# Token gather and scatter of a mixture-of-experts step: one-hot picks in f32 replaced by rounded high and low parts

## The chip, the cores and the metric

The kernel runs on one core of a Trainium2 chip. The metric is the device time of one execution in microseconds (us). Before the change, three runs gave 1468.37 us as the median, from 1468.09 to 1469.5.

## What is computed

One inference step of a two-layer decoder for two request groups that share weights: a prompt of 256 tokens and eight single sample tokens, so 264 tokens in all (T = 264), with 1024 features each. Layer 0 is a gated MLP with a causal mixing over chunks, layer 1 a differential attention; behind each stands a mixture of 16 experts, of which a token uses two. Every part ends in a residual and a layer norm. The part that matters here, cut from the reference:

```
h = x * (1 + sc2) + sh2                                   # modulation from a conditioning vector
scores = softmax(h @ router_w);  sel = scores + router_bias
# the group of 4 experts whose two best sel sum highest; in it the two best experts
gate = the two scores, divided by their sum, at their experts; 0 elsewhere     # (264, 16)
a = silu(h @ w_gate[e]) * (h @ w_up[e]) * gate[:, e]      # for every expert e, width 512
f = sum over e of a @ w_down[e]
x = layer_norm(alpha * x + (1 + g2) * f)
```

All inputs and outputs are float32.

## The kernel before

Activations stand with features on the partitions: a tensor such as `hT` is 128 x 8 x 264, eight blocks of 128 features. TensorE (PE) makes products into PSUM, ACT copies them out, VectorE (DVE) does the elementwise work, SyncE (SP) issues the weight loads, GpSimd (POOL) little. Each engine has its own program, written out by hand in its order; counters on semaphores order the engines among themselves. No planner takes part.

**Rounded products.** TensorE's f32 matmul has two matmul rows in the trace; a matmul of two rounded operands (the type fp32r) has one. Wherever weights are multiplied, the kernel splits both operands into a rounded high part, which ACT makes by a copy into a rounded tile, and a rounded low part, which DVE makes as the difference, and adds three products: high x high, high x low, low x high. The gather and the scatter of the experts don't do so: they are f32.

**Stages of one expert layer** (`moe`, in each engine's program). The modulation writes `hT`. TensorE makes the router's logits (L563), transposes them, computes the tile of one later modulation vector (`ada_tile`, L490), and turns `hT` into token rows by transposes (`turned`, L402), six groups of up to four blocks, which ACT copies to `tokA`. Meanwhile DVE selects the experts. From the selection TensorE counts the tokens of each expert by small matmuls (`small`, L425), and so each token gets two slots among 2 x 264 = 528: the slots are sorted by expert. `ada_turn` (L425 too) puts the columns of a finished modulation vector on the partitions; ahead of the gather two such turns run in each layer, and in layer 0 a tile `ada_tile(1, 0, 2)` between them.

DVE makes the one-hot table `pick` (L1689 and L1693): for token t and slot s it is 1 where s is one of t's slots. The *gather* (L599 to L603) multiplies token rows by `pick` in 16 groups, two halves of the slots times eight feature blocks; a group is three f32 matmuls over 128, 128 and 8 tokens, with 264 columns. Its result `xg` holds the features of every slot in expert order, with padding behind.

The experts run in a loop, two to a turn (L659 to L664), each over 128 slots from its first one on. For an expert `part` makes the gate and up products (L620, rounded, in four quarters), DVE and ACT the gated activation, TensorE turns it (L422), and `down` (L639, f32) the down projection of the expert before; ACT copies the result to `yg`, feature blocks by slots. `yg` lies in the buffer `reg2`, which POOL clears at the start of the layer (L1100 to L1103). The weights stream through a ring of six slots of 2 MB (`wring`), which SP loads in one fixed order, each as soon as the slot's last reader is done.

If an expert had more than 128 tokens, all engines would run a further loop (`more_pe` L687, its counterparts on ACT, DVE and SP); every engine reads a flag to a register and branches (on TensorE L691 and L692, on DVE L1604). With the inputs here the body is skipped.

*The tail of the layer.* Behind the last down projection stand, in this order: the wait for ACT, the flag and branch, the transposes of each token's two slot numbers and two gates (`sg`, L422), four spreads of those rows over all partitions (L425) that DVE copies to `sgB`, ten `turned` groups that turn `yg` into slot rows (L402), which ACT copies to `yr`, in layer 0 the tile `ada_tile(1, 1, 0)`, and the *scatter* (L682 to L684): eight groups of five f32 matmuls, over four times 128 and once 16 slots, slot rows times the table `put`. DVE builds `put` in fifteen operations (L1764 to L1771): per block of 128 slots, the gate where the slot is the token's first, plus the gate where it is the second.

```
put[:, k, :] = (sgB[:, 0, :] == mine) * sgB[:, 2, :]
rs[:]        = (sgB[:, 1, :] == mine) * sgB[:, 3, :]
put[:, k, :] = put[:, k, :] + rs[:]
```

Then come in layer 0 one modulation turn and one tile, the residual (DVE scales `xT` first, L1491), and the norm: a sum over features by matmuls (L457), centring (L1510), squares by ACT and their sum, scaling. In layer 0 a turn and a tile lie between the two sums, and DVE does two weight splits of the next projection (`tile_split`, L1477, 2048 elements each) between centring and scaling. That projection, `kv` in layer 0, is L391 with three rounded products per block.

Helpers that these steps share: `group` (L381) opens one of the PSUM banks `pj` and runs a list of matmuls, `evac` on ACT (L1129) copies a bank out, `low` and `high` split expert weights (L1702 on DVE, L1233 on ACT), L1738 multiplies the two halves of an expert's activation.

## Time and profile before

| | |
|---|---|
| runs, median (lowest to highest) | 1468.37 us (1468.09 to 1469.5) |
| the profiled execution, its own time | 1468.32 us |
| its span, from first to last instruction | 1466.5 us |
| TensorE busy | 1273.1 us, 87% of the span |
| VectorE busy | 815.9 us, 56% |
| ScalarE busy | 549.8 us, 37% |
| GpSimd busy | 21.2 us, 1% |
| chain that ended last, by engine | PE 74%, DVE 16%, ACT 3%, issue 2%, DMA 2%, SPq 2% |

Shares of busy time are means over stages of different kinds, so the stages have to be read one by one. The chain of waits follows the work back from the last instruction, at each step to what released it; "issue" in it is time in which an engine waited for nothing that the profile shows. PEclk in a stretch is the granted TensorE clock as a share of 2.4 GHz: 1.00 is 2.4 GHz and 0.50 is 1.2 GHz, values between are stretches with both. An engine's name with a q at its end is its sequencer, PEld the weight loads of TensorE.

### The profile page before, as it was taken

What the parts mean: (1) busy time and instruction counts of PE and PEld (TensorE: products, weight loads), DVE (VectorE), ACT (ScalarE), POOL (GpSimd) and SP (SyncE); (2) the same over time, 40 slices, a digit from 0 to 9 for tenths busy, and PEclk for the clock granted to TensorE, in tenths of its full rate; (3) what the DMA queues carried; (4) which work ended last, traced back from release to release, by engine and by line L of the source; (5) the groups of instructions that cost most, each with busy time, mean ns of one, the idle gap of its engine ahead of it and who ended that gap; (6) DMA issues with size and microseconds to landing.
All of it is one profiled execution on the core that took longest, in us unless ns stands there. A gap on an engine that the chain in (4) does not pass through costs nothing.

```text
span 1466.5 us, 19316 instructions
## 1 busy us (share of the span) xinstructions
PE 1273.1 (87%) x7246; PEld 997.5 (68%) x7246; DVE 815.9 (56%) x970; ACT 549.8 (37%) x663; POOL 21.2 (1%) x26
## 2 busy tenths in 40 slices
PE   4797879899999997899877886676998999999985
PEld 1695745788888885599543443264657888888864
DVE  1436472666666632645599989366316666666334
ACT  1333224555555522353322221133125555555321
POOL 2000010000000000000000000001000000000000
PEclk9899979999999998999856556678559999999988
DMA  9939530999999966534469999853009999999200
GB/s 332 387 114 337 177 111 19 347 336 338 340 338 338 339 235 235 180 125 158 179 222 341 353 342 346 301 214 116 1 0 342 336 337 335 334 335 335 108 2 30
DMA packets 143713, 355.40 MB, mean 242 GB/s; under 512 B 4706, under 2 KB 4899, under 8 KB 143652
## 3 DMA queue, kind: packets, MB, share of 16 engines
q1 hardware_dynamic: 142388, 350.98, 67.4%
q0 software_dynamic: 1264, 3.59, 0.8%
q8 instruction: 40, 0.66, 0.2%
q14 instruction: 21, 0.17, 0.0%
HBM read 351.28 MB, written 3.28 MB: 242 GB/s over the span
## 4 chain that ended last, share of the span: by engine, by line
PE 74%; DVE 16%; ACT 3%; issue 2%; DMA 2%; SPq 2%; ACTq 0%; DVEq 0%
PE gu L620 24%; PE pj L391 20%; PE pj L639 16%; DVE reg L1843 3%; PE tb L425 3%; DVE wring L1840 3%; PE gu L457 2%; PE gu L807 2%; PE tb L422 2%; PE gu L809 1%; DMA wring<-in_a_w_in 1%; SPq L912 1%; PE pj L490 1%; DVE yT L1851 1%; PE pj L402 1%
## 5 line engine op out<-in xcount | busy, mean ns | idle before, releaser
L1702 DVE TENSOR_TENSOR wlo<-wring,whi 128x2048 fp32r<-128x2048 f32 x128 | 290.2, 2289 | 103.7 <-ACT whi L1233 103.6
L1233 ACT ACTIVATE whi<-wring 128x2048 fp32r<-128x2048 f32 x128 | 244.7, 1916 | 144.5 <-PE gu L620 144.5
L639 PEld LDWEIGHTS pj<-tokB,wring 128*128 128x128 f32 x2048 | 233.4, 192 | 4.7 <-issue 2.1
L639 PE MATMUL pj<-tokB,wring 128*128 128x128 f32 x2048 | 233.9, 275 | 1.7 <-issue 1.7
L1129 ACT ACTIVATE reg<-pj 128x264 f32<-128x264 f32 (+2 forms) x168 | 83.9, 510 | 365.2 <-PE pj L391 147.6
L620 PE MATMUL gu<-whi,xhi 128*128 128x512 f32 x512 | 207.7, 406 | 12.9 <-DVE xlo L1728 12.9
L620 PE MATMUL gu<-wlo,xhi 128*128 128x512 f32 x512 | 204.6, 400 | 0.0
L620 PE MATMUL gu<-whi,xlo 128*128 128x512 f32 x512 | 204.4, 399 | 0.0
L620 PEld LDWEIGHTS gu<-whi,xhi 128*128 128x128 f32 x512 | 98.2, 192 | 35.7 <-DVE xlo L1728 7.9
L620 PEld LDWEIGHTS gu<-whi,xlo 128*128 128x128 f32 x512 | 98.1, 192 | 23.2
L620 PEld LDWEIGHTS gu<-wlo,xhi 128*128 128x128 f32 x512 | 98.1, 192 | 21.6
L1728 DVE TENSOR_TENSOR xlo<-reg,xhi 128x1024 fp32r<-128x1024 f32 x32 | 39.2, 1226 | 115.0 <-ACT xhi L1237 115.0
L391 PE MATMUL pj<-yT,tok 128*128 128x264 f32 (+1 forms) x192 | 79.4, 559 | 0.6 <-issue 0.6
L391 PE MATMUL pj<-yT_rounded,wlo 128*128 128x264 f32 x256 | 74.6, 291 | 0.0
L1840 DVE TENSOR_TENSOR wring<-wring,yT 128x2048 f32<-128x2048 f32 x32 | 73.2, 2288 | 2.0 <-ACT yT L1129 1.5
L1843 DVE TENSOR_REDUCE reg<-wring 128x32 f32<-128x2048 f32 x32 | 73.2, 2286 | 1.1
L490 PE MATMUL pj<-wring,cT 128*32 128x512 f32 x384 | 55.7, 708 | 18.9 <-DMA wring<-in_ada_w 18.0
L391 PEld LDWEIGHTS pj<-yT,tok 128*128 128x128 f32 (+1 forms) x192 | 42.3, 253 | 36.7 <-issue 32.4
L1738 DVE TENSOR_TENSOR tokB<-tokB,gu 128x512 f32<-128x512 f32 x32 | 22.0, 688 | 60.0 <-PE gu L620 60.0
L797 PE MATMUL pj<-wring,reg 128*32 128x512 f32 x256 | 51.9, 963 | 1.6 <-DVE lamx L1901 1.6
L1477 DVE TENSOR_TENSOR wlo<-wring,half_reg 128x2048 fp32r<-128x2048 f32 x14 | 32.1, 2290 | 37.3 <-ACT half_reg L1158 37.3
L1129 ACT ACTIVATE yT<-pj 128x264 f32<-128x264 f32 (+1 forms) x48 | 21.3, 459 | 81.4 <-PE pj L391 75.6
(295 smaller groups left out, 1732.1 us busy)
## 6 DMA issues: line engine op xcount, KB each, us to landing
wring<-in_moe_w_gate SPq DMA_DIRECT2D x32, 2048.0 KB, 9.4
wring<-in_moe_w_up SPq DMA_DIRECT2D x32, 2048.0 KB, 10.0
wring<-in_moe_w_down SPq DMA_DIRECT2D x32, 2048.0 KB, 9.0
wring<-in_ada_w SPq DMA_DIRECT2D x24, 2048.0 KB, 13.8
wring<-in_cache_k SPq DMA_DIRECT2D x64, 512.0 KB, 5.0
wring<-in_cache_v SPq DMA_DIRECT2D x64, 512.0 KB, 5.0
wring<-in_a_w_in SPq DMA_DIRECT2D x4, 2048.0 KB, 19.9
wring<-in_a_w_out SPq DMA_DIRECT2D x2, 2048.0 KB, 16.4
```

Of the source, the lines that this page charges most:

```text
L391: m = pe.matmul(out, lhsT, rhs, start=(j == 0), stop=(j == len(pairs) - 1))
L425: return lambda dst: pe.matmul(dst, lhsT, rhs, start=start, stop=stop)
L490: m = pe.matmul(bank[32 * j:32 * j + 32, 0:512], cT[:, k, :], w[:, k, :], start=(half == 0), stop=(half == 1))
L620: m = pe.matmul(gu[q // 2][:, :], x[:, c, :], w[:, k, :], start=(c == 0 and n == 0), stop=(c == C - 1 and n == 2))
L639: m = pe.matmul(bank[:, i * P:(i + 1) * P], w[:, k, f * P:(f + 1) * P], aT[:, k, :], start=(k == 0), stop=(k == FB - 1))
L797: m = pe.matmul(pj[2 + n][32 * p:32 * p + 32, :], sW[:, s % 4, 4 * k + p, :], wring[:, slot, p * D + n * 512:p * D + (n + 1) * 512], start ...
L1129: act.activation(dst, bank[0:rows, 0:n] if n < 512 or rows < P else bank[:, :].rearrange("p (f n) -> p f n", n=P), func, scale=scale).then ...
L1233: act.activation(whi[q], quarter(wring, q, s), ACT.Copy).then_inc(hi_ready, 1)
L1702: dve.tensor_tensor(quarter(wlo, q, s), quarter(wring, q, s), whi[q].bitcast(F32), ALU.subtract).then_inc(lo_ready, 1)
L1728: dve.tensor_tensor(xlo, xg[:, :, bass.ds(first, P)], xhi.bitcast(F32), ALU.subtract).then_inc(xe_ready, 1)
L1840: link(dve.tensor_tensor(keys.rearrange("p (g n) -> p g n", g=2), keys.rearrange("p (g n) -> p g n", g=2), qbc[:, s % 2:s % 2 + 1, :].to_b ...
L1843: i = dve.tensor_reduce(sS[:, s, g0:g0 + 2, :].rearrange("p g x -> p (g x)").unsqueeze(2), keys.rearrange("p (x d) -> p x d", d=HD), AX.X, ...
```

## The change

*Gather.* ACT copies each pair of blocks of `hT` to a rounded tile `hhi`, and DVE writes the difference to `hlo`. `turned` still turns `hT` itself, and ACT copies these rows to rounded tiles `gR`; six more `turned` groups turn `hlo`, and ACT copies those to `gl` and `gls`. The table `pickR` is rounded (it holds zeros and ones). A group of the gather now has six matmuls, high and low part of each of the three token blocks, all of rounded operands.

*Slot numbers and gates.* The transposes of `sg` and TensorE's read of the flag move ahead of the experts. Slot number and gate of the first choice are spread after the last expert's gate and up products, ahead of its `down`, those of the second choice behind `down`; then comes TensorE's branch. DVE compares the spread rows straight out of PSUM with each partition's slot number: `putR` becomes a rounded table of zeros and ones, and the gate of each slot is summed to a column `gcol`.

*Scatter.* ACT copies the turned slot rows out of PSUM times `gcol`, to rounded tiles `yrR`; DVE makes the low part from the same bank, bank times gate minus `yrR`. `turned` waits for DVE's low part four groups back. A group of the scatter has ten matmuls of rounded operands. The tile `ada_tile(1, 1, 0)` waits for the seventh low part, the scatter for all ten.

*Beside.* POOL's clear of `reg2` waits for the end of the gather, and ACT waits for it after the first expert. In layer 0 the turns and tiles behind the scatter each move one place later: turn 1 and tile 2 between the sums of the norm, turn 2 and tile 3 behind the norm. Of the two weight splits of the next projection, on ACT the first moves ahead of the scatter's fourth eviction and the second behind the norm; on DVE one stays between centring and scaling and the other moves behind the norm and the split of the projection's input. The multi-pass branch's buffer `piece` moves to `ws2`.

```diff
...
...
-yr = reg1[:, 0:NK * D].rearrange("p (k n) -> p k n", n=D)
-pick = yT[:, :, :].rearrange("p c t -> p (c t)")[:, 0:3 * SLOT_N].rearrange("p (j n) -> p j n", n=SLOT_N)
-put = hT[:, :, :].rearrange("p c t -> p (c t)")[:, 0:NK * T].rearrange("p (k t) -> p k t", t=T)
-piece = hT[:, :, :].rearrange("p c t -> p (c t)")[:, 0:2048].rearrange("p (b k n) -> p b k n", b=2, n=P)
+gR = rounded("tokens_high", "tok4", 0, 3 * D).rearrange("p (j n) -> p j n", n=D)
+gl = rounded("tokens_low", "tokB", 0, 2 * D).rearrange("p (j n) -> p j n", n=D)
+gls = rounded("sample_low", "reg2", 0, D)
+hhi = rounded("mod_high", "reg2", 0, C * T).rearrange("p (c t) -> p c t", t=T)
+hlo = sqT
+pickR = rounded("pick_rounded", "yT", 0, 3 * SLOT_N).rearrange("p (j n) -> p j n", n=SLOT_N)
+putR = rounded("put_rounded", "hT", 0, NK * T).rearrange("p (k t) -> p k t", t=T)
+yrR = rounded("rows_high", "reg1", 0, NK * D).rearrange("p (k n) -> p k n", n=D)
+lowA = rounded("rows_low_a", "tok4", 0, 3 * D).rearrange("p (k n) -> p k n", n=D)
+lowB = rounded("rows_low_b", "tokB", 0, 2 * D).rearrange("p (k n) -> p k n", n=D)
+piece = ws2[:, :, :].rearrange("p c t -> p (c t)").rearrange("p (b k n) -> p b k n", b=2, n=P)
 flatB = tokB[:, :, :].rearrange("p b n -> p (b n)")
 aT = flatB[:, 0:512].rearrange("p (f n) -> p f n", n=P)
 atok = flatB[:, 512:1024]
 upT = flatB[:, 1024:1536].rearrange("p (f n) -> p f n", n=P)
-sgB = flatB[:, 0:4 * T].rearrange("p (i t) -> p i t", t=T)
...
+def slots_of(k):
+    return P if k < NK - 1 else LAST
+def row_low(k):
+    return lowA[:, k, :] if k < 3 else lowB[:, k - 3, :]
...
+        at[f"modulated{l}"] = op.n
...
+        operand()
+        for n, j in ((NB, 2), (P, 0), (P, 1)):
+            for q in range(2):
+                turned(n, hlo[:, 4 * q:4 * q + 4, j * P:j * P + n])
...
             for c in range(C):
-                group(P, T, [(tokA[0:n, j, c * P:(c + 1) * P], pick[0:n, j, half * T:(half + 1) * T])
-                             for j, n in enumerate(tiles)])
+                group(P, T, [(x[0:n, c * P:(c + 1) * P], pickR[0:n, j, half * T:(half + 1) * T])
+                             for j, n in enumerate(tiles) for x in (gR[:, j, :], gl[:, j, :] if j < 2 else gls)])
...
+        small([((6, P * j, n), tr(sg[0:n, j, :], n)) for j, n in enumerate(tiles)])
+        pe.wait_ge(routed, l + 1)
+        many = pe.value_load(starts[0:1, 3 * NE:3 * NE + 1], min_val=0, max_val=1)
...
-        def down(s, turn):
...
-            emptied()
+            pe.wait_ge(tb_evac, b.value(later))
...
...
         for s in range(SLOTS):
             loads[s] += 16 * 6
         step(3)
-        down(2, 0)
+        def spread_rows(i):
+            small([((P, 0, T), mm(ident[0:4, i:i + 1].to_broadcast([4, P]), lgT[0:4, :]))])
+        for i in (0, 2):
+            spread_rows(i)
+        down(2, 0, 2)
+        for i in (1, 3):
+            spread_rows(i)
+        at[f"moe{l}_main"] = g.n
+        more_pe(l, many, g.n)
         pe.wait_ge(pj_evac, g.n)
-        at[f"moe{l}_main"] = g.n
-        more_pe(l)
-        small([((6, P * j, n), tr(sg[0:n, j, :], n)) for j, n in enumerate(tiles)])
-        emptied()
-        for i in range(4):
-            small([((P, 0, T), mm(ident[0:4, i:i + 1].to_broadcast([4, P]), lgT[0:4, :]))])
-        for k in range(NK):
-            n = P if k < NK - 1 else LAST
-            for q in range(2):
-                turned(n, yg[:, 4 * q:4 * q + 4, k * P:k * P + n])
-        pe.wait_ge(pj_evac, g.n)
+        at[f"rows_bank{l}"] = banks[0]
+        for n in range(2 * NK):
+            k, q = divmod(n, 2)
+            if n >= NBANK:
...
+        rows_out = g.n
+        pe.wait_ge(rows_low, 2 * NK * (l + 1) - 3)
         if l == 0:
             ada_tile(1, 1, 0)
-        operand()
+        pe.wait_ge(pj_evac, rows_out)
+        pe.wait_ge(rows_low, 2 * NK * (l + 1))
+        pe.wait_ge(gates_ready, l + 1)
         for c in range(C):
-            group(P, T, [(yr[0:(P if k < NK - 1 else LAST), k, c * P:(c + 1) * P], put[0:(P if k < NK - 1 else LAST), k, :])
-                         for k in range(NK)])
+            cols = slice(c * P, (c + 1) * P)
+            group(P, T, [(x[0:slots_of(k), cols], putR[0:slots_of(k), k, :])
+                         for k in range(NK) for x in (yrR[:, k, :], row_low(k))])
         at[f"moe{l}_end"] = g.n
...
+    def more_pe(l, many, main):
         m = more[l]
-        pe.wait_ge(routed, l + 1)
-        many = pe.value_load(starts[0:1, 3 * NE:3 * NE + 1], min_val=0, max_val=1)
         with pe.If(many):
+            pe.wait_ge(pj_evac, main)
             x, p_, ev = Tally(m["x"]), Tally(m["piece"]), Tally(m["evac"])
...
     moe(0)
-    ada_turn(1, 1)
-    ada_tile(1, 2, 1)
     def beside():
-        ada_turn(1, 2)
-        ada_tile(1, 3, 3)
+        ada_turn(1, 1)
+        ada_tile(1, 2, 1)
     norm(yT, beside)
+    ada_turn(1, 2)
+    ada_tile(1, 3, 3)
...
-        pool.wait_ge(tb_evac, at[f"router{l}"])
+        pool.wait_ge(pj_evac, at[f"moe{l}"])
         pool.memset(reg2[:], 0.0).then_inc(yg_clear, 1)
...
+        act.activation(dst, bank[0:rows, 0:n] if n < 512 or rows < P or len(dst.shape) == 2 else bank[:, :].rearrange("p (f n) -> p f n", n=P), func, scale=scale).then_inc(pj_evac, 1)
...
+        for p in range(4):
+            act.wait_ge(op_ready, at[f"modulated{l}"] - 3 + p)
+            act.activation(hhi[:, 2 * p:2 * p + 2, :], hT[:, 2 * p:2 * p + 2, :], ACT.Copy).then_inc(mod_high, 1)
...
-                evac_wide(tokA[0:n, j, q * 512:(q + 1) * 512], n)
+                evac_wide(gR[0:n, j, q * 512:(q + 1) * 512], n)
+        for n, x in ((NB, gls), (P, gl[:, 0, :]), (P, gl[:, 1, :])):
+            for q in range(2):
+                evac_wide(x[0:n, q * 512:(q + 1) * 512], n)
...
-        act.wait_ge(yg_clear, l + 1)
...
+        act.wait_ge(yg_clear, l + 1)
...
+        act.wait_ge(gates_ready, l + 1)
         for k in range(NK):
-            n = P if k < NK - 1 else LAST
+            n = slots_of(k)
             for q in range(2):
-                evac_wide(yr[0:n, k, q * 512:(q + 1) * 512], n)
+                evac(yrR[0:n, k, q * 512:(q + 1) * 512], rows=n, n=512, scale=gcol[0:n, 2, k:k + 1])
...
             evac(yT[:, c, :])
+            if l == 0 and c == 3:
+                tile_split()
     moe(0)
-    for _ in range(2):
-        tile_split()
-    rows(1, 2)
-    norm(yT[:], lambda: rows(1, 3))
+    norm(yT[:], lambda: rows(1, 2))
+    tile_split()
+    rows(1, 3)
     source_split("kv", xT, 4)
     rows(1, 4)
...
+        for p in range(4):
+            two = slice(2 * p, 2 * p + 2)
+            dve.wait_ge(mod_high, 4 * l + p + 1)
+            i = dve.tensor_tensor(hlo[:, two, :], hT[:, two, :], hhi[:, two, :].bitcast(F32), ALU.subtract)
+        ready(i)
...
-                i = dve.tensor_scalar(pick[:, j, half * T:(half + 1) * T], iota, sg[:, j, s0:s0 + 1], None, ALU.is_equal)
+                i = dve.tensor_scalar(pickR[:, j, half * T:(half + 1) * T], iota, sg[:, j, s0:s0 + 1], None, ALU.is_equal)
...
+        empty(dve.tensor_copy(lgT[0:6, :], batch()[0:6, 0:T]))
+        last_empty()
...
+        spare = tok4[:, 2:4, :].rearrange("p j n -> p (j n)")
+        gate = spare[:, NK * T:(NK + 1) * T]
+        for i in range(2):
+            dve.wait_ge(tb_done, tbe.value() + 2)
+            slot = tb[tbe.n % 2][:, 0:T]
+            link(dve.tensor_copy(gate, tb[(tbe.n + 1) % 2][:, 0:T]))
+            for k in range(NK):
+                mine = kst[:, K_PART + k:K_PART + k + 1]
+                if i == 0:
+                    dve.tensor_scalar(putR[:, k, :], slot, mine, None, ALU.is_equal)
+                else:
+                    dve.scalar_tensor_tensor(putR[:, k, :], slot, mine, putR[:, k, :].bitcast(F32), ALU.is_equal, ALU.add)
+            for k in range(NK):
+                mine = kst[:, K_PART + k:K_PART + k + 1]
+                j = dve.scalar_tensor_tensor(spare[:, k * T:(k + 1) * T], slot, mine, gate, ALU.is_equal, ALU.mult, accum_out=gcol[:, i, k:k + 1])
+            j.then_inc(tb_evac, 2)
+            tbe.add(2)
+            last_empty()
+        dve.tensor_tensor(gcol[:, 2, :], gcol[:, 0, :], gcol[:, 1, :], ALU.add).then_inc(gates_ready, 1)
+        dve.wait_ge(gates_ready, l + 1)
         gp.n = at[f"moe{l}"]
         dve.wait_ge(pj_evac, gp.add(2 * NE))
...
-        empty(dve.tensor_copy(lgT[0:6, :], batch()[0:6, 0:T]))
-        for i in range(4):
-            empty(dve.tensor_copy(sgB[:, i, :], batch()[:, 0:T]))
-        last_empty()
-        for k in range(NK):
-            mine = kst[:, K_PART + k:K_PART + k + 1]
-            dve.scalar_tensor_tensor(put[:, k, :], sgB[:, 0, :], mine, sgB[:, 2, :], ALU.is_equal, ALU.mult)
-            link(dve.scalar_tensor_tensor(rs[:], sgB[:, 1, :], mine, sgB[:, 3, :], ALU.is_equal, ALU.mult))
-            i = dve.tensor_tensor(put[:, k, :], put[:, k, :], rs[:], ALU.add)
-            if k < NK - 1:
-                link(i)
-        ready(i)
-        if l == 0:
-            mod_rows(1, 1)
+        for n in range(2 * NK):
+            k, q = divmod(n, 2)
+            rows, cols = slots_of(k), slice(q * 512, (q + 1) * 512)
+            dve.wait_ge(pj_evac, gp.add())
+            dve.scalar_tensor_tensor(row_low(k)[0:rows, cols], pj[(at[f"rows_bank{l}"] + n) % NBANK][0:rows, :], gcol[0:rows, 2, k:k + 1],
+                                     yrR[0:rows, k, cols].bitcast(F32), ALU.mult, ALU.subtract).then_inc(rows_low, 1)
...
     def beside():
-        mod_rows(1, 2)
-        for _ in range(2):
-            tile_split()
+        mod_rows(1, 1)
+        tile_split()
     norm(yT[:], xT, V_LNG + 8, V_LNB + 8, beside, True)
     source_split("kv", xT)
+    tile_split()
+    mod_rows(1, 2)
```

## Rows read from the trace of the kernel before

**Rows 1.** Chain of waits, whole span: start us, us, what.

```profile
212.75 27.50 PE pj L391 x96
...
575.88 20.92 PE pj L391 x80
...
1035.87 51.79 PE pj L391 x96
```

**Rows 2.** Stretches: us, length; busy PE, PEld, DVE, ACT, POOL; PEclk; DMA; GB/s.

```profile
201.00:202.00 1.00, 0.38 (x6) 0.30 (x6) 0.49 (x3) 0.00 (x0) 0.00 (x0) 0.67 1.02 422
211.00:212.00 1.00, 1.00 (x7) 0.31 (x3) 0.96 (x4) 0.10 (x1) 0.00 (x0) 0.71 0.00 0
230.00:235.00 5.00, 5.00 (x18) 2.75 (x18) 0.00 (x0) 1.11 (x3) 0.00 (x0) 1.00 0.00 0
1045.00:1060.00 15.00, 15.00 (x30) 7.87 (x28) 0.00 (x0) 1.95 (x5) 0.00 (x0) 0.50 0.00 0
```

**Rows 3.** Timeline, router of layer 0: start us, us, engine line operation out<-in.

```profile
195.36 2.78 PE L402 MATMUL pj<-kst,hT 128*8 128x128 f32 x24
...
206.36 1.88 PE L425 MATMUL tb<-kst,tok 128*128 128x9 f32 x8
...
208.17 3.59 PE L490 MATMUL pj<-wring,cT 128*32 128x512 f32 x16
```

**Rows 4.** Chain of waits, 535 to 625 us, the tail of layer 0.

```profile
545.84 7.40 PE pj L639 x64
...
553.96 7.19 issue
...
562.35 3.89 PE tb L425 x8
...
573.96 1.93 PE pj L490 x16
...
605.45 2.55 DVE yT L1510 x4
...
608.10 4.40 DVE wlo L1477 x2
```

**Rows 5.** Chain of waits, 1380 to 1466 us, the tail of layer 1.

```profile
1392.41 7.40 PE pj L639 x64
...
1438.34 3.77 PE gu L457 x16
...
1442.22 0.72 DVE yT L1510
```

**Rows 6.** Lines L691, L692, L1604: count, min/median/max ns, first and last start us.

```profile
L691 PEldq TENSOR_LOAD <-starts x2: 313/401/489, 554.0 to 1400.6; - x2
...
L692 PEldq COMPARE_BRANCH  x2: 3418/4830/6243, 554.8 to 1401.2; - x2
...
L1604 DVEq COMPARE_BRANCH  x2: 63/63/63, 554.6 to 1401.2; - x2
```

**Rows 7.** Rounded and f32 matmuls: two stretches, four timeline rows.

```profile
628.00:634.00 6.00, 6.00 (x52) 6.00 (x51) 3.55 (x4) 2.81 (x5) 0.00 (x0) 1.00 0.00 0
624.00:625.00 1.00, 1.00 (x8) 1.00 (x8) 1.00 (x7) 0.69 (x2) 0.00 (x0) 0.70 0.00 0
...
620.47 0.42 PE L391 MATMUL pj<-s_rounded,half_ws 128*128 128x264 f32 x1
...
620.69 0.42 PE L391 MATMUL pj<-yT_rounded,wlo 128*128 128x264 f32 x1
...
1014.11 0.15 PEld L563 LDWEIGHTS tb<-hT,rw 128*16 128x16 f32 x1 [0.29 <-issue]
...
1014.55 0.14 PEld L563 LDWEIGHTS tb<-hT,rw 128*16 128x16 f32 x1 [0.29 <-DVE hT L1463]
```

**Rows 8.** Lines L1766, L1738: count, min/median/max ns, first and last start us; form.

```profile
L1766 DVE SCALAR_TENSOR_TENSOR hT<-tokB,kst x10: 494/494/496, 566.7 to 1415.9; 128x264 f32<-128x264 f32 x10
...
L1738 DVE TENSOR_TENSOR tokB<-tokB,gu x32: 686/687/690, 258.2 to 1384.1; 128x512 f32<-128x512 f32 x32
```

More of the change, by code:

```diff
@@ L217, in build @@
         selR = sb("selR", [P, NB], F32R)
+        gcol = sb("gcol", [P, 3, NK])
         abT = reg1[:, 0:2 * C * T].rearrange("p (c t) -> p c t", t=T)
@@ L339, in build @@
         rotary_in = sem("rotary_in")
+        mod_high = sem("mod_high")
+        gates_ready = sem("gates_ready")
+        rows_low = sem("rows_low")
         routed = sem("routed")
@@ L623, in part, with down @@
                     used.add()
-                def down(s, turn):
+                def down(s, turn, later=0):
                     loaded(s, turn=turn)
                     w = wring[:, s, :].rearrange("p (k n) -> p k n", n=D)
-                    emptied()
+                    pe.wait_ge(tb_evac, b.value(later))
                     for d in range(2):
@@ L679, in moe @@
+                for n in range(2 * NK):
+                    k, q = divmod(n, 2)
+                    if n >= NBANK:
+                        pe.wait_ge(rows_low, 2 * NK * l + n - NBANK + 1)
+                    turned(slots_of(k), yg[:, 4 * q:4 * q + 4, k * P:k * P + slots_of(k)])
+                rows_out = g.n
+                pe.wait_ge(rows_low, 2 * NK * (l + 1) - 3)
                 if l == 0:
                     ada_tile(1, 1, 0)
-                operand()
+                pe.wait_ge(pj_evac, rows_out)
@@ L685, in moe @@
                 at[f"moe{l}_end"] = g.n
-            def more_pe(l):
+            def more_pe(l, many, main):
                 m = more[l]
-                pe.wait_ge(routed, l + 1)
-                many = pe.value_load(starts[0:1, 3 * NE:3 * NE + 1], min_val=0, max_val=1)
                 with pe.If(many):
+                    pe.wait_ge(pj_evac, main)
                     x, p_, ev = Tally(m["x"]), Tally(m["piece"]), Tally(m["evac"])
@@ L1128, in evac @@
                 act.wait_ge(pj_done, g.add())
-                act.activation(dst, bank[0:rows, 0:n] if n < 512 or rows < P else bank[:, :].rearrange("p (f n) -> p f n", n=P), func, scale=scale).then_inc(pj_evac, 1)
+                act.activation(dst, bank[0:rows, 0:n] if n < 512 or rows < P or len(dst.shape) == 2 else bank[:, :].rearrange("p (f n) -> p f n", n=P), func, scale=scale).then_inc(pj_evac, 1)
             def evac_wide(dst, rows):
@@ L1688, in moe @@
                     for j in range(3):
-                        i = dve.tensor_scalar(pick[:, j, half * T:(half + 1) * T], iota, sg[:, j, s0:s0 + 1], None, ALU.is_equal)
+                        i = dve.tensor_scalar(pickR[:, j, half * T:(half + 1) * T], iota, sg[:, j, s0:s0 + 1], None, ALU.is_equal)
                     link(i)
                     for j in range(3):
-                        at_h = pick[:, j, half * T:(half + 1) * T]
-                        i = dve.scalar_tensor_tensor(at_h, iota, sg[:, j, s0 + 1:s0 + 2], at_h, ALU.is_equal, ALU.add)
+                        at_h = pickR[:, j, half * T:(half + 1) * T]
+                        i = dve.scalar_tensor_tensor(at_h, iota, sg[:, j, s0 + 1:s0 + 2], at_h.bitcast(F32), ALU.is_equal, ALU.add)
                     ready(i)
```

## The prediction

> **What bounds the kernel now.** I read the page first, then the chain of waits over the whole span, then the same chain, the timeline and the busy time by stage around the two places that the change touches. The chain is held by TensorE for three quarters of the span; in the chain the reader is to find long blocks of line 391 that are neither dense projections nor experts [rows 1]. The blocks at 212.75 and 1035.87 gather token columns into expert slots; the one at 575.88, and one like it in layer 1 that ends before 1438.34, scatter slot rows back. The same 96 rows of the gather (16 groups of 3 f32 matmuls, each matmul two rows) take 27.50 us in layer 0 and 51.79 us in layer 1. The reason is the clock: in layer 0 it falls to 0.50 (1.2 GHz) at 201.3, after TensorE had stood idle from 198.1 on, and comes back to 1.00 (2.4 GHz) at about 211.6, when the modulation tile of line 490 is nearly through; in layer 1 there is no such tile and the gather runs at 0.50 to its end [rows 2, 3]. Both stretches have no weight traffic (DMA 0.00 in both rows), so the experts start as much earlier as the gather ends earlier.
>
> The second place is the tail after the last expert. In layer 0 its last down projection ends at 553.24, then 7.19 us pass with TensorE waiting for nothing shown, then slot numbers are spread (3.89), rows turned, a modulation tile (1.93) and the scatter (20.92 in the chain) follow one another, and the centring of the norm starts only at 605.45 [rows 1, 4]. In layer 1 the same steps run from 1399.81 to 1442.22 [rows 1, 5]. The 7.19 us are a register load and a branch: the branch alone takes 6.24 us in layer 0 and 3.42 us in layer 1 [rows 6].
>
> **Price of one matmul.** At 1.00, 52 rounded 264-column matmuls fit in 6.00 us: 0.115 each. At 0.50 they start 0.22 apart; f32 rows start 0.44 apart at 0.50, so 0.22 at 1.00 [rows 7]. A group of the old gather takes 27.50/16 = 1.72 at 1.00, that is 6 x 0.22 + 0.40, and 51.79/16 = 3.24 at 0.50, 6 x 0.44 + 0.60. The scatter's group takes 20.92/8 = 2.61 = 10 x 0.22 + 0.41. I charge the rest (0.40 and 0.60) to the two changes between 128 and 8 (or 16) rows in each group; the new groups keep two such changes, so I keep the rest whole. New gather group: 6 x 0.115 + 0.40 = 1.09 at 1.00, 6 x 0.22 + 0.60 = 1.92 at 0.50; sixteen of them 17.5 or 30.7 us. New scatter group: 10 x 0.115 + 0.41 = 1.56 at 1.00, 2.8 at 0.50; eight 12.5 or 22.4. Without the rest the gather would be 11.0 and 21.1, the scatter 9.2 and 17.6: ends of the range.
>
> **Which clock the gathers get.** This decides most. The nearest row is layer 1's own gather: at 0.50 it stayed there for 51.8 us [rows 1, 2], with TensorE at work all the time; the new group has the same changes between row counts, with half the column passes between them. So a gather that starts at 0.50 I take to stay. Layer 1 starts so: the position matmuls and two modulation turns before it are small, and nothing like the tile comes. In layer 0 the six added turns of the low part (as the first six, 24 rows, 2.78 us [rows 3], paced by ACT's evictions) keep TensorE at work until about 200.6, so the fall comes later, among the position matmuls; these then run partly faster, the tile starts some 2 us earlier, and it ended only 0.2 us after the rise before. I take it that the rise is missed and that layer 0 gathers at 0.50 too: slightly the likelier of two.
>
> The Trainium skill (TensorE: Matmul & The Clock Gate, Part 1) says that the throttled state is the default and that sustained matmul work releases it, without asking what kind of matmul. Layer 1's gather of 51.8 us speaks against it here, the projection at 620 for it; by that rule both gathers would be at full clock soon, and the sum would be that of the second rival below.
>
> **Term 1, layer 0 gather: +2.8.** 30.7 - 27.5 = +3.2 for the matmuls; +0.9 for the modulation turn behind it at 0.50 (a turn took 1.88 there [rows 3], half at 1.00); -1.3 because the position matmuls run partly at 1.00 (0 to -4). Hidden: the split of the modulated tokens (ACT 4 copies, DVE 4 subtractions) lies beside the router's logits, the low turns and six evictions beside the selection chain of DVE, the transposes of the slot columns and the register load beside ACT's and DVE's first token split. If that cover fails, each costs up to about 1 us.
>
> **Term 2, layer 1 gather: -23.1.** 30.7 - 51.8 = -21.1, and -2.0 (0 to -4) for the earlier start.
>
> **Term 3, layer 0 tail: -20.6.** Two spreads now stand before the last down projection; at 1.00 they cost 2 x 0.49 (four took 3.89 at 0.50 [rows 4]), and the first lies beside DVE's copy of the last transposes: +0.5 (0 to 1.9). Down ends 553.7, the other two spreads 554.7. DVE's second half of the tables: a copy and an add, 0.4 each, five picks at 0.40 to 0.49 and five sums at 0.45 to 0.65 (the old pick took 0.49, a 128x512 one out of PSUM 0.69 [rows 8]): 5.4 (4.7 to 6.5), so gates at 560.1. The branch stays, but TensorE's queue reaches it while the matmuls still run and it ends near 559, beside the tables (if it is reached only behind the spreads: +1 here, 0 in layer 1). Now the rows: DVE's register load and branch, 0.6 as an estimate (TensorE's load 0.49, DVE's branch 0.06 [rows 6]), ACT's first eviction, then ten low parts on DVE, 128x512 out of PSUM at 0.69 [rows 8]: 567.8. They are late next: the turns wait for them, four banks deep. The modulation tile starts with the seventh low part, so the scatter starts at 568.6 (567.8 to 570.5) instead of 575.8: the ten dense turns before it raised the clock in both layers, and I take 1.00. With 12.5 it ends at 581.1 instead of 596.8: -15.7. From there to the centring 8.65 us passed, since DVE scaled the residual only after the turn behind the scatter; in layer 1, where it did so beside the scatter, 3.88 [rows 5]: -4.75. One weight split of the two, 4.40 together [rows 4], leaves the norm; the statistic of the squares is late next, so I take -0.15 (0 to -2.2). The split and the modulation behind the norm then lie beside the first projection, and the two loads that wait for the tiles (slots 0 and 1) are issued earlier, not later.
>
> **Term 4, layer 1 tail: -11.3.** Down ends 1400.3, spreads 1401.3, gates 1406.7, low parts 1414.4, scatter 1414.5 to 1427.0 against 1438.34 [rows 5].
>
> POOL's clear of 4.5 us moves behind the gather; its result is wanted only after an expert's work, and the next job in POOL's queue, the rotary load, waits for later things: 0. Sum: 2.8 - 23.1 - 20.6 - 11.3 = -52.2. The profiled execution has 1466.5 between first and last instruction and 1468.32 in all; this is within 0.05 of the median 1468.37. 1468.3 - 52.2 = **1416**.
>
> **The rivals.**
> - Layer 0 keeps or regains 2.4 GHz, layer 1 not: layer 0's term is 17.5 - 27.5 - 1.3 = -11.3, the sum -66: 1402. For it: it did so before; against: the shifted tile.
> - Both gathers come to 2.4 GHz. At the projection the rise came at 624.6, some 4.2 us after its first matmuls [rows 7]; 4.2 us at 0.50 (2.2 groups) and 13.8 groups at 1.09 make 19.3: 11.4 saved twice, and the turn: 1392 (1389 where they start at full). For it: the projection's rows; against: layer 1's old gather.
> - The tail is longer. A scatter at 0.50 costs 9.9 more per layer: 1426, or 1436 for both. And DVE's branch now stands on the path: its 0.06 us [rows 6] becomes 3.4 to 6.2 if it pays what TensorE's pays: 1426 for both layers. By the Trainium skill (Runtime: NRT & Kernel Launch, Instruction fetch mechanics) a taken branch beyond the pages already fetched stalls for its target; TensorE's two branches agree, DVE's do not, perhaps since its skipped body is short.
> - Slower: the picks don't run in a single pass. If a pick on rounded tiles cost what an f32 one does (0.57 in layer 0's gather, 1.08 in layer 1's, 0.52 in the scatters), the doubled count would make 55, 104, 42 and 42 us against 30.7, 30.7, 12.5 and 12.5: +156, 1572. It turns slower from 0.15 us per matmul above my price (52.2 over 352). Against it: every rounded 264-column row [rows 7].
>
> **Chances.** Forecast 0.44, its own range 1408 to 1424; first rival 0.22; second 0.16; longer tail 0.14; slower 0.03; no gain for a reason not seen 0.01. The range 1390 to 1432 takes in the first rival, most of the second and most of the tail. 0.2% is 2.9 us, about what this kernel's runs can tell: faster 0.96, same 0.01, slower 0.03.
>
> **What would show it.** The granted clock in the two gather stretches (0.50 or 1.00) and their length, 30.7 or 17.5 to 19; the scatter's clock and 12.5; ten low parts in a row at 0.69 with TensorE waiting for them; the branch beside the tables; centring 3.9 after the scatter. A gather group far from 1.92 or 1.09, or low parts that TensorE doesn't wait for, would make the sum wrong.

## The result and the profile after

The changed kernel takes 1418.19 us as the median of four runs (1411.54, 1412.13, 1424.25, 1428.71), the kernel before 1468.93; the ratio is 0.9669, with a 95% interval from 0.9618 to 0.972. The forecast was 1416. A ratio here compares only runs within 1.5% of the fastest of the same kernel. The runs lie in two groups, though, and a run of each has a trace: the first took 1412.13 us (span 1410.4), the second, of the same changed kernel run again (experiment 1), 1424.13 (span 1422.4). The table sets the forecast's terms against both, by the same landmarks in each trace.

| stretch, us | before | first trace | second trace | forecast |
|---|---|---|---|---|
| start to layer 0's first expert product | 244.69 | 236.16: -8.5 | 248.11: +3.4 | +2.8 |
| experts of layer 0, to the last down's end | 308.53 | 309.14: +0.6 | 309.15: +0.6 | in the next |
| from there to the `kv` projection | 66.90 | 45.42: -21.5 | 45.43: -21.5 | -20.6 |
| `kv` to layer 1's first expert product | 471.17 | 445.39: -25.8 | 445.36: -25.8 | -23.1 |
| experts of layer 1 | 308.50 | 308.36: -0.1 | 308.41: -0.1 | in the next |
| last down's end to the end | 66.68 | 65.89: -0.8 | 65.90: -0.8 | -11.3 |
| sum | 1466.5 | 1410.4: -56.1 | 1422.4: -44.1 | -52.2 |

The chain of waits over the span of the first trace (columns as in [rows 1], whose three rows and [rows 5] they answer to; L391 is now L407):

```profile
213.91 17.81 PE pj L407 x96
...
559.40 12.89 PE pj L407 x80
...
1001.55 30.67 PE pj L407 x96
...
1359.15 21.60 PE pj L407 x80
1380.75 5.39 PE gu L473 x16
```

The same view of the second trace:

```profile
212.35 30.51 PE pj L407 x96
...
571.37 12.89 PE pj L407 x80
...
1013.49 30.67 PE pj L407 x96
...
1371.14 21.59 PE pj L407 x80
```

The reader is to see that one program did the same gather of layer 0 in 17.81 and in 30.51 us, and the same scatter in 12.89 (layer 0) and 21.60 (layer 1). Busy time by stretches (columns as in [rows 2]) names the reason; of the first trace:

```profile
215.00:220.00 5.00, 5.00 (x28) 3.77 (x28) 4.86 (x11) 3.57 (x7) 0.00 (x0) 1.00 0.00 0
1010.00:1020.00 10.00, 10.00 (x33) 7.39 (x32) 0.61 (x1) 1.95 (x5) 0.00 (x0) 0.50 0.01 2
1362.00:1372.00 10.00, 10.00 (x38) 8.34 (x37) 2.28 (x8) 1.17 (x3) 0.00 (x0) 0.50 0.01 2
```

and of the second:

```profile
215.00:220.00 5.00, 5.00 (x17) 3.58 (x16) 4.15 (x2) 0.99 (x4) 0.00 (x0) 0.50 0.00 0
```

TensorE is busy all the time in each row, at 1.00 (2.4 GHz) or at 0.50 (1.2 GHz). In the first trace the clock rose to 1.00 at 213.22, just ahead of the gather; in the second it had fallen at 204.74 and stayed at 0.50 to 252.5. The Trainium skill (TensorE: Matmul & The Clock Gate, Part 1) says that the gate watches activity free of the program, so that one kernel rises at another place in another run; the two traces fit that (a rise at 213.22 in one, none up to 252.5 in the other), though the gather itself also begins 1.6 us apart in them (213.77 and 212.20).

The tail of layer 0 in the first trace, as the chain of waits from 520 us shows it, and TensorE's branch by its source line (columns as in [rows 6]):

```profile
546.96 2.09 DVE put_rounded L1816 x5
549.05 2.08 DVE tok L1819 x10
...
552.59 4.09 DVE rows_low_a L1835 x6
...
557.40 1.93 PE pj L506 x16
...
L725 PEldq COMPARE_BRANCH  x2: 3729/4987/6245, 543.6 to 1342.8; - x2
```

The branch still takes 6.2 and 3.7 us, but starts at 543.6, under the down projection that ends at 545.30, and ends beside the tables. Behind it come the tables, the low parts at 0.68 each, the tile, the scatter, in the order that was forecast. From the scatter's end to the centring 3.88 us pass (576.17 less 572.29), as forecast.

### The profile page after: what moved, and what is told of

Its sections match the earlier page's. It is cut to its first block, busy times and chain, and to the rows that moved or that the text cites. A ratio compares the mean times of both kernels' runs of the same rounds, so it can differ in the third digit from the quotient of the medians.

```text
span 1410.4 us, 19510 instructions
## 1 busy us (share of the span) xinstructions
PE 1231.2 (87%) x7294; PEld 991.6 (70%) x7294; DVE 836.1 (59%) x1026; ACT 562.3 (40%) x683; POOL 20.8 (1%) x26
## 4 chain that ended last, share of the span: by engine, by line
PE 70%; DVE 13%; SPq 7%; issue 4%; ACT 2%; DMA 2%; ACTq 0%; DVEq 0%
PE gu L644 25%; PE pj L407 17%; PE pj L663 16%; PE tb L441 3%; PE gu L473 3%; SPq L1076 3%; SPq L1074 3%; DMA wring<-in_ada_w 2%; PE tb L438 2%; PE pj L506 2%; DVE reg L1907 1%; DVE wring L1904 1%; DVE yT L1915 1%; SPq L1073 1%; DVE wlo L1521 1%
## 5 line engine op out<-in xcount | busy, mean ns | idle before, releaser
L1164 ACT ACTIVATE reg<-pj 128x264 f32<-128x264 f32 (+2 forms) x148 | 73.3, 497 | 305.7 <-PE pj L663 145.1
L407 PE MATMUL pj<-yT_rounded,wlo 128*128 128x264 f32 x256 | 74.1, 289 | 0.0
L407 PE MATMUL pj<-hT_rounded,half_reg 128*128 128x264 f32 x160 | 47.9, 299 | 2.2 <-DVE u_rounded L1530 2.2
L407 PEld LDWEIGHTS pj<-yT_rounded,wlo 128*128 128x128 f32 x256 | 49.6, 194 | 0.0
L832 PE MATMUL pj<-wring,reg 128*32 128x512 f32 x256 | 47.2, 883 | 1.6 <-DVE lamx L1965 1.6
```

What stands on the lines that cost most here:

```text
L407: m = pe.matmul(out, lhsT, rhs, start=(j == 0), stop=(j == len(pairs) - 1))
L832: m = pe.matmul(pj[2 + n][32 * p:32 * p + 32, :], sW[:, s % 4, 4 * k + p, :], wring[:, slot, p * D + n * 512:p * D + (n + 1) * 512], start ...
L1164: act.activation(dst, bank[0:rows, 0:n] if n < 512 or rows < P or len(dst.shape) == 2 else bank[:, :].rearrange("p (f n) -> p f n", n=P), ...
```

## The experiments

Each run stands beside runs of the kernel before on the same chip; their medians there were 1467.19 (first four experiments), 1467.01 (next three) and 1469.09 (last two).

**1. The changed kernel again** (no edit).

> The changed kernel once more, unaltered, for its spread and a second trace. Theory (the clock): the matmuls cost what they were priced at, and what differs from run to run is the clock that TensorE is granted in three stretches, the gather of layer 0 and the two scatters. Then the times spread again from about 1411 to 1429; a gather of layer 0 takes either 17.8 us at 1.00 or about 30.7 at 0.50, a scatter 12.9 or 21.6, and the difference of two runs is the sum of such differences. Rival (transfers): the gathers and scatters take the same in each run, and the spread comes from weight or cache transfers between them.

Six runs, 1426.04 median: 1411.85, 1413.38, then 1424.13 to 1429.89. The traced one is the second trace above: gather of layer 0 at 0.50, 30.66 us from its first matmul to its end against 17.95; all other stretches are within 0.1 us of the first trace. The 12.0 us between the two spans are the gather's clock (12.7 us, and 0.8 for the modulation turn behind it), less the 1.6 us by which the gather began earlier. That is the theory's case; the rival, transfers, fails on these two traces. The runs of 1428 to 1430 have no trace; their mean granted clock is lower still (0.862 to 0.868, against 0.877 in the second trace and 0.881 in the first), and which stretch that is stays open.

**2 and 3. One half of the change each.** The first keeps the old tail, the second the old gather.

```diff
 2: +group(P, T, [... six rounded matmuls ...])      # gather, splits, turns, clear as changed
    -small([((6, P * j, n), tr(sg[0:n, j, :], n)) ...]) ahead of the experts, putR, gcol, yrR, row_low
 3: the reverse
```

> The gather alone is changed (rounded parts, six more turns, the clear of POOL moved); the tail is the old one. By the terms read from the two traces: layer 1 gather -21.1 and 2 us later start by the subtractions on VectorE in each layer; layer 0 gather -9.7 at 1.00 or +3 at 0.50. So 1438 to 1442 where layer 0 gathers at 1.00, 1451 to 1455 where not, beside 1468. If the gather's gain depended on the new tail, this run would stay within 5 us of 1468.

> The tail alone is changed (tables beside the last expert, gates by the eviction, rounded scatter, the moved turns and splits); the gather is the old one. Layer 0 from the last down projection to the next dense projection -21.5 (66.9 to 45.4), layer 1 between -2.3 (scatter at 0.50) and -11 (at 1.00): 1436 to 1446. The 3.4 us that attention was shorter in the first trace come here too if they belong to the tail (the earlier loads), and in the gather-only kernel if not.

The gather alone gives 1443.77 (ratio 0.9819, 0.978 to 0.9857), in two groups again, 1432.59 and 1434.91, and 1441.64 to 1447.67; its trace is one of the second group, with both gathers at 0.50. Both groups lie below what was expected (1438 to 1442 and 1451 to 1455), by 3 to 9 us from the lower ends. I had charged a start 2 us later in each layer, and neither layer shows it (from the router's last matmul to the first one on the selected experts 8.68 us in both, before 8.94); and attention was 3.2 us shorter in this trace. The tail alone gives 1453.2 (0.9906, 0.988 to 0.9932), 1450.98 to 1456.56. So -23.4 and -14.0, together -37.4, and -41.2 was measured for both in the same comparison: the halves add up to within 4 us, and the two groups come with the new gather. The chain rows of both:

```profile
214.61 30.51 PE pj L399 x96
580.98 20.92 PE pj L399 x80
1036.15 30.66 PE pj L399 x96
1396.09 20.96 PE pj L399 x80
```

```profile
213.08 27.50 PE pj L402 x96
573.98 12.90 PE pj L402 x80
1022.22 51.79 PE pj L402 x96
1401.77 21.44 PE pj L402 x80
```

The tail-only kernel missed its range: 1436 to 1446 was expected, and it took 1453.2. Most of the miss is in layer 0's tail, 51.2 us from the last down projection to `kv` where the whole change takes 45.4. Behind the spreads TensorE waits for nothing shown:

```profile
555.19 9.22 issue
```

Its branch runs from 552.4 to 558.6, one weight load follows, and the next comes only at 564.41, so the turns start late. In both traces of the whole change the turns follow right behind the branch. That the branch lies beside the tables is therefore true of the changed kernel as it stands and not of its tail alone; what holds TensorE behind the branch, the runs don't show.

The scatter of layer 1 is at 0.50 here too, where the old f32 one ran at 1.00 and took 20.96: the new scatter has as many matmul rows, each half as long, and takes longer. The time from `kv` to the next layer's dense projection doesn't follow the change: 345.2 us in the gather-only kernel, 349.2 in the tail-only one, 348.4 before, 345.2 after. Over all eleven traces it lies between 345.0 and 349.2, at 348.9 in the changed kernel of experiment 5 and at 345.9 in the old one of experiment 8. What sets it I did not test.

**4. Unread matmuls ahead of the gathers and in the tails.**

```diff
+def warm(n): n times pe.matmul(gu[1][:, 0:256], ident, kst[:, K_MASK:K_MASK + 256], ...)
+warm(6) ahead of the wait for key; warm(3) twice among parts; warm(8) behind small(parts)
+warm(8) behind more_pe; layer 1: warm(8) ahead of the scatter
```

> The changed kernel with work added that nobody reads: f32 matmuls of 256 columns into an idle PSUM bank, ahead of the router's position sums, among them and behind them (20 in each layer), 8 behind the branch in each tail, 8 ahead of layer 1's scatter. Clock theory: both gathers at 1.00 (17.8), both scatters at 1.00 (12.9): -13 and -8.7 against the first trace, the added matmuls that stand on the path cost 1 to 3 us a layer, so 1391 to 1398, and the spread between runs falls below 4 us. Rival (the clock of these stretches is set by their own mix of short matmuls, whatever stands before): the gather of layer 1 stays at 30.7 and the scatter at 21.6, and the time rises by 3 to 8 us.

1418.4, far from 1391 to 1398, and the runs spread over 13 us (1408.83 to 1422.12), not under 4. Layer 1's scatter came to 1.00 (13.00 us from first to last matmul, against 21.60), but its gather took 29.78. The timeline shows TensorE ahead of it, and the stretches show the clock:

```profile
1010.58 3.72 PE L576 MATMUL gu<-kst 128*128 128x256 f32 x16
1014.14 1.85 PE L441 MATMUL tb<-kst,tok 128*128 128x9 f32 x16
1015.84 0.37 PE L407 MATMUL pj<-pick_rounded,tokens_high 128*128 128x264 f32 x1
1016.05 0.28 PE L407 MATMUL pj<-pick_rounded,tokens_low 128*128 128x264 f32 x1
1016.16 0.28 PE L407 MATMUL pj<-pick_rounded,tokens_high 128*128 128x264 f32 x1
1016.28 0.28 PE L407 MATMUL pj<-pick_rounded,tokens_low 128*128 128x264 f32 x1
1016.50 0.38 PE L407 MATMUL pj<-pick_rounded,tokens_high 8*128 8x264 f32 x1
1016.72 0.28 PE L407 MATMUL pj<-pick_rounded,sample_low 8*128 8x264 f32 x1
1016.93 0.51 PE L407 MATMUL pj<-pick_rounded,tokens_high 128*128 128x264 f32 x1
```

```profile
1016.00:1017.00 1.00, 1.00 (x7) 0.72 (x7) 0.96 (x4) 0.00 (x0) 0.00 (x0) 1.00 0.00 0
1018.00:1028.00 10.00, 10.00 (x33) 7.60 (x32) 5.72 (x11) 1.95 (x5) 0.00 (x0) 0.50 0.00 0
```

The added matmuls in front of a wait weren't free either: in layer 0 those behind the branch took 5.41 us, 3.42 of them at 0.50, and the scatter began 18.0 us after the last down projection instead of 14.1. The gather of layer 1 was entered at 1.00 and lost it at 1017.05, 1.2 us in; what stood right before was the two modulation turns of 9-column matmuls (1.85 us). The rows of 8 partitions also show their price: at 1.00 the steps are 0.12 between full matmuls and 0.21 to 0.22 around the two thin ones.

**5. Zero rows instead.** Every matmul of gather and scatter over 128 partitions.

```diff
-group(P, T, [(x[0:n, c * P:(c + 1) * P], pickR[0:n, j, ...]) ...
+group(P, T, [(x[:, c * P:(c + 1) * P], pickR[:, j, ...]) ...
+pool.memset(gR[:, 2, :], 0.0); pool.memset(gls, 0.0)       # and ACT's waits for them
-return P if k < NK - 1 else LAST
+return P
```

> The changed kernel with every gather and scatter matmul over 128 partitions: the tile of the 8 sample tokens and the block of the last 16 slots are filled up with zero rows (two clears more on GpSimd, 1 us each). The work is larger by rows, the same by matmuls. Theory: the rest of each group (0.40 us at 1.00, 0.60 at 0.50) is the change between row counts, and the thin matmuls also keep the clock low. Then a gather takes 16 x 6 x 0.115 = 11.0 us at 1.00; one that starts at 0.50 rises within some 4 us, as the dense projection did, and takes about 13 in place of 30.7; the scatters 9.2, or about 13 where they start low. Against the first trace: -7, -17, -4 and -9, so about 1375, and the spread from the gather of layer 0 shrinks to 3 us. Rival (the rest is the change of PSUM bank and the wait for its eviction): groups stay at 1.11 and 1.92 us, the clock stays where it was, 1411 to 1429.

1374.46 (1372.22 to 1379.27, a spread of 7 us and not 3), 0.9366 of before with an interval from 0.9348 to 0.9384, and 44 us below the changed kernel's 1418.19 (52 below the 1426.04 of experiment 1). The trace is of the run of 1379.27. From first to last matmul: gathers 12.83 and 13.46, scatters 10.02 and 11.53. The stretches of layer 1's gather and two rows of its timeline:

```profile
999.00:1001.00 2.00, 2.00 (x11) 2.00 (x10) 1.77 (x7) 0.39 (x1) 0.00 (x0) 0.50 0.00 0
1003.00:1011.00 8.00, 8.00 (x68) 8.00 (x68) 4.31 (x2) 4.30 (x11) 0.00 (x0) 1.00 0.01 2
```

```profile
999.49 0.42 PE L408 MATMUL pj<-pick_rounded,sample_low 128*128 128x264 f32 x1
999.71 0.42 PE L408 MATMUL pj<-pick_rounded,tokens_high 128*128 128x264 f32 x1
```

It starts at 0.50 at 998.25 and rises at 1001.78. The matmul of the sample rows takes the step of every other, 0.22 at 0.50. At 1.00 a scatter group takes 10.02/8 = 1.25 against 12.89/8 = 1.61, so 0.36 of the 0.41 that I had charged to the changes between row counts are theirs, or the thin matmuls' own.

**6. Unread matmuls in other places.**

```diff
+warm(4) among parts; layer 1: warm(4) behind small(parts), warm(6) between ada_turn(l, 11) and the gather,
+warm(6) behind more_pe, warm(8) ahead of the scatter
```

> Unread f32 matmuls again, put elsewhere: 4 among the position sums of each layer; in layer 1 alone 4 behind them, 6 between the two modulation turns and the gather, 6 behind the branch of its tail, 8 ahead of its scatter. The run with 20 a layer kept 1.00 up to layer 1's gather and lost it 1.2 us into it, right behind the two turns (9 columns a matmul). Clock theory: the gather keeps the clock that the work just before it earned, so with full matmuls between turns and gather both gathers run at 1.00 (17.9) and layer 1's scatter too (13.0): -12.7 and -8.6 against the first trace, +1 a layer for those on the path: 1391 to 1396, spread below 4 us. Rival (a gather lowers its own clock): layer 1's gather falls to 0.50 again within 4 us of its start and takes 28 to 31; 1404 to 1410.

1410.97 (1407.66 to 1412.97). In layer 1 both came out as the clock theory had it:

```profile
1023.07 17.72 PE pj L407 x96
...
1370.71 12.66 PE pj L407 x80
```

That speaks against the rival: this gather entered at 1.00, with full matmuls just ahead, and kept it to its end (18.06 us from first to last matmul). The price was 3.6 us (from the selection's end to the gather 11.1 us against 7.5). In layer 0, which got no such matmuls right ahead of its gather, the clock rose at 213.63 and fell again at 217.04, 2.6 us after the gather's first matmul, and the gather took 28.80. A modulation turn stood right ahead of it; one also stood ahead of layer 0's gather in the first trace, which had entered 0.55 us after a rise and kept 1.00 to its end. So full matmuls just ahead were enough in layer 1; whether a gather keeps the clock without them differs between these traces, and nothing here shows what decides it. The time stayed above the 1396 expected by layer 0's 11 us and that price.

**7. The kernel before with these matmuls ahead of its f32 gathers** (the gather part of the edit of 6).

> The kernel before with the same unread matmuls ahead of its two f32 gathers (4 in layer 0, 14 in layer 1), its tail untouched. Clock theory: the f32 gather of layer 1 runs at 1.00 too, 27.7 in place of 51.8, for 1 us on the path of each layer: -22, so about 1446. So half of what the change saves on layer 1's gather would have been the clock's to give. Rival (a gather lowers its own clock): 1469 to 1472.

1475.35 is the median of twelve runs in two groups: six from 1459.15 to 1467.87, six from 1482.82 to 1492.07. The lower group is at 0.9979 of before (0.9958 to 0.9999), where 1446 was expected. The upper group has no trace. That of a run of the lower group (1461.89):

```profile
1035.55 3.60 PE gu L560 x8
...
1042.11 3.71 PE gu L560 x8
...
1049.04 5.32 PE gu L560 x12
1054.35 0.70 PE pj L391 x2
```

The f32 gather of layer 1 did run at 1.00 (27.86 us from first to last matmul), but here the clock had fallen at 1034.26, and the added matmuls ran at 0.50: 12.6 us on the path where I had priced 1, half of the 23.9 that the gather gave. Layer 0's tail, which the edit leaves alone, was 5.2 us longer in this trace (72.1 against 66.9), most of it a second wait of TensorE behind the branch (4.60) as in experiment 3.

**8. The kernel before with the zero rows only.**

```diff
-group(P, T, [(tokA[0:n, j, ...], pick[0:n, j, ...]) ...
+group(P, T, [(tokA[:, j, ...], pick[:, j, ...]) ...
+pool.memset(tokA[:, 2, :], 0.0)
-P if k < NK - 1 else LAST                  # slot rows, their eviction, the scatter
+P
```

> The kernel before, all f32, with only the zero rows: its gathers and scatters run over 128 partitions in every matmul. From the filled run of the changed kernel: a group keeps 0.11 us beside its matmuls, and a gather that starts at 0.50 rises within 4 to 7 us. So 16 x (6 x 0.22 + 0.11) = 22.9 us for the gather of layer 0 (27.7), some 25 for that of layer 1 (51.8), 8 x (10 x 0.22 + 0.11) = 18.5 for a scatter (21.0): -5, -27 and twice -2.5, about 1430. Rival (f32 matmuls in two rows don't raise the clock of a gather, rounded ones do): layer 1's gather stays at 0.50 and takes about 44; 1449.

1424.04 (1423.6 to 1426.37), 0.9692 (0.9667 to 0.9718): with no rounded part, no new table and the old tail, this is about the changed kernel's time (0.9669 and 0.9696 of before), and its runs lie within 3 us. Its chain rows:

```profile
213.26 21.46 PE pj L392 x96
569.71 18.00 PE pj L392 x80
1023.11 23.97 PE pj L392 x96
1376.25 18.04 PE pj L392 x80
```

An f32 gather raises its clock as a rounded one does (0.50 up to 1027.89, then 1.00), so the kind of the matmul isn't what kept the old gather of layer 1 at 0.50 for 51.8 us; with its thin matmuls filled up, it was at 0.50 for 4.8. The zero rows do a second thing, which the other three stretches show at 1.00 before and after: layer 0's gather goes from 27.65 to 21.61 us, each scatter from 21.0 to 18.1, by the steps around the thin matmuls alone.

**9. Zero rows and 8 unread matmuls ahead of layer 1's scatter.**

> The filled version of the changed kernel with 8 unread f32 matmuls in layer 1 where TensorE waits for the last low parts, ahead of the scatter. In its trace the clock fell to 0.50 there at 1339.7 and the scatter took 11.5 against 10.0 in layer 0. Clock theory: 10.0 and a start no later, -1.5, and the norm's first sum follows at 1.00: 1371 to 1374, at the limit of what five rounds can tell; the trace decides. Rival: the added matmuls push the scatter back by what they save.

1375.63 (1373.11 to 1380.26), no different from 1374.46. The scatter took 10.13 in place of 11.53, but began 15.9 us after the last down projection in place of 14.6, and ended 26.1 us after it in both: the rival was right, what it saves it costs. In this trace both filled gathers start at 0.50; each rises 3.8 us in and takes 13.59.

## Why the prediction was right, and where only in sum

**The price of one matmul was right.** The gather group at 0.50 was forecast at 1.92 us and took 30.66/16 = 1.92, at 1.00 1.09 and 17.95/16 = 1.12; the scatter group 1.56 and 1.61. Picks on rounded tiles run in a single pass; the slower rival fails on that. So was it right that a gather which starts at 0.50 stays there (30.67 us in layer 1 in both traces), on which the second rival fails. The prediction had this from the old gather only; experiments 5, 8 and 9 show what it hung on here: with the thin matmuls filled up, such gathers rise within 5 us. The charge for the changes between row counts was right too: 0.36 of its 0.41 us for a scatter group go with the thin matmuls.

**Layer 0's gather was a toss, as it was put.** The rise that I took to be missed was missed in the second trace (+3.4 for the term, forecast +2.8) and met in the first (-8.5, the first rival's case: forecast -11.3). The 2.8 us between -8.5 and -11.3 lie ahead of all that the change touches: the router's first matmul came at 189.74 there, at 187.69 in the second trace of the same program and at 186.89 before. From that matmul to the gather's first one 24.0 and 24.5 us passed, before 25.7, so the -1.3 held (-1.7 and -1.2). That case came with the rival's clock, not with its time, since layer 1's scatter went the other way.

**Layer 0's tail was right step by step.** Spreads, gates (6.0 us behind the last down projection, forecast 6.4), low parts (0.68 each), the branch beside the tables, the tile behind the seventh low part, the scatter at 1.00; from the scatter's end to `kv` 18.43 us (forecast 23.32 - 4.75 - 0.15 = 18.42). VectorE's branch in its new place took 0.06 us, so that rival fell. Two readings of the prediction are slightly off, without effect on its sum: the lowest and highest of its terms for the second half of the tables add up to 5.05 to 6.5 us, not 4.7 to 6.5 (4.82 was measured), and the rise at 624.6 came 4.5 us after `kv`'s first matmul at 620.12, not 4.2.

**The step that failed is term 4.** I took layer 1's scatter to run at 1.00, for "the ten dense turns before it raised the clock in both layers". They did raise it, at 1356.68, but TensorE then stood idle from 1357.24 to 1359.15 for the last two low parts, with no modulation tile to fill that wait as in layer 0:

```profile
1354.67 2.57 PE L418 MATMUL pj<-kst,reg 128*128 128x128 f32 x13
1359.15 0.36 PE L407 MATMUL pj<-put_rounded,rows_high 128*128 128x264 f32 x1 [1.91 <-DVE rows_low_b L1835]
```

The clock fell again at 1360.1, and the scatter took 21.60 instead of 12.5; the norm's first sum behind it 5.39 instead of 3.77. This is the rival of the longer tail, for one layer, and was given 0.14. Experiment 6 shows the cause: with unread matmuls behind the branch and in that wait the scatter took 13.01, and from the last down projection to the scatter's end 29.15 us against 36.28. Experiment 9, with them in that wait alone, on top of the zero rows, has its scatter at 1.00 from end to end, where experiment 5 fell to 0.50 at 1339.7.

**The other 2.7 us** of the stretch from `kv` on are mostly attention (from `kv`'s start to the next layer's dense output projection 3.2 us less than before), not gather: the gather itself gave 21.1, as forecast, and what lies just ahead of it some 1.7 of the 2.0.

So 1416 lies between two groups of runs, near 1412 and 1427, rather than on one: the failed term (+10.5) and either outcome of layer 0 make -44 or -56. In the first trace the failed term was made up for by the rise in layer 0 and by attention, neither of which the forecast had. That the median of four runs, two of each group, came out 2 us from 1416 is luck; the six of experiment 1 have 1426.04. The chance that I gave to one clock per gather would better have been given to a kernel that has both.

**Where the gain comes from.** The chip granted the old gather of layer 1 half its clock, and the change makes its rows half as long without touching that: 51.8 to 30.7. Experiment 8 keeps the f32 rows and fills up the thin ones, which brings the clock up and shortens the steps: 51.8 to 24.0. Experiment 5 has both. The filled kernel goes below the second rival's 1392, which had both gathers at full clock, since its groups are also shorter (0.80 us at 1.00 in place of 1.12).

## What to carry to other kernels

Look at the granted clock of a stretch before counting its matmuls: a TensorE that the profile shows busy all the time can be at 0.50, and a stretch with the same number of rows, each half as long, can take longer than the old one did (layer 1's scatter, 21.60 us against 20.96). Fill a matmul over a few partitions up with zero rows where these stand between full ones; it cost one or two clears of 0.95 us a layer here and gave 44 us to the changed kernel and 45 to the one before, nearly as much as the change itself (51). Where the time of a kernel falls in groups, take more than one trace before believing a single span.

## What the runs showed of the hardware

- Thin matmuls are not cheaper but dearer: around one over 8 partitions rounded matmuls of 264 columns step at 0.21 to 0.22 us at 1.00, between those over 128 at 0.12 (experiment 4).
- A stretch with two thin matmuls in six can stay at 0.50 to its end with TensorE busy throughout (30.7 us rounded, 51.8 f32); filled up, it rose 3.5 and 3.8 us (rounded, experiments 5 and 9) and 4.8 us (f32, experiment 8) after its start. The profile models the ends of matmuls, so "busy throughout" doesn't exclude short gaps between them. Whether it is the thin matmuls' few partitions or the longer steps around them that the clock goes by, no run separates.
